# Odd layer's sample outputs in four column strips, with one transpose as a step of its own

## The reference

```python
def mix_odd(x, s_ret, start, w_in, w_out):
    z = x @ w_in
    q = rotate_xpos(z[..., :o1] ...); k = rotate_xpos(z[..., o1:o2] ...) * (DK_C ** -0.5)
    v = z[..., o2:o3].reshape(B, L, H_C, DV_C); g = z[..., o3:]
    ...
    o, s_new = chunked_linear_attention(q, k, v, log_a, s_ret, RET_CHUNK)
    o = rms_norm(o).reshape(B, L, MIX_C) * jax.nn.silu(g)
    return o.astype(x.dtype) @ w_out, s_new
```

## Time and profile before

| | us |
|---|---|
| three runs | 1682.03, 1676.82, 1681.51 |
| median | 1681.51 |
| span of the profiled execution | 1678.0 |

### The profile page before, as it was taken

How to read it: one execution, slowest core, us unless ns; L and a number is a source line. 1 busy time by engine, 2 the same in 40 slices (tenths; PEclk the granted TensorE clock), 3 DMA queues, 4 the chain that set the end, 5 groups by cost and what they waited for, 6 DMA issues and landing times.

```text
span 1678.0 us, 21821 instructions
## 1 busy us (share of the span) xinstructions
PE 1597.4 (95%) x7950; PEld 808.1 (48%) x7950; DVE 539.5 (32%) x1320; ACT 340.2 (20%) x689; POOL 144.5 (9%) x221
## 2 busy tenths in 40 slices
PE   8999899999999999999999999989999999999998
PEld 5784544434444443446665755554443444443343
DVE  2235622222222222351343335371222222222225
ACT  2101222211112211231222222012122112221122
POOL 0330100000000000000011011010000000000000
PEclk9969999999999999999999999989999999999999
DMA  9623789999989999953465586587999998999970
GB/s 301 241 82 133 276 335 419 420 420 420 420 354 420 420 420 420 383 205 134 163 238 207 183 282 219 191 322 292 420 421 420 420 419 357 422 420 421 419 294 29
DMA packets 119270, 536.09 MB, mean 319 GB/s; under 512 B 17848, under 2 KB 29368, under 8 KB 69407
## 3 DMA queue, kind: packets, MB, share of 16 engines
q1 hardware_dynamic: 95975, 470.35, 69.8%
q0 software_dynamic: 21360, 61.64, 10.2%
q10 hardware_dynamic: 1872, 3.22, 0.5%
HBM read 526.15 MB, written 23.87 MB: 328 GB/s over the span
## 4 chain that ended last, share of the span: by engine, by line
PE 82%; DMA 11%; DVE 3%; issue 2%; ACT 1%; SPq 1%; POOL 0%; ACTq 0%; DVEq 0%
PE ps L1244 23%; PE ps L1108 12%; PE ps L1086 12%; DMA weights<-in_w_exp_up 11%; PE ps L1258 10%; PE ps L1220 5%; PE ps L1237 3%; PE ps L1216 2%; PE ps L1251 1%; PE ps L1008 1%; PE ps L1097 1%; PE ps L1278 1%; PE ps L986 1%; PE ps L899 1%; PE ps L999 1%
## 5 line engine op out<-in xcount | busy, mean ns | idle before, releaser
L1244 PE MATMUL ps<-weights,x_feat 128*64 128x512 f32 x1984 | 437.8, 593 | 36.5 <-DMA weights<-in_w_exp_up 18.1
L1244 PEld LDWEIGHTS ps<-weights,x_feat 128*64 128x64 f32 x1984 | 147.1, 137 | 320.5 <-issue 317.9
L1258 PE MATMUL ps<-weights,arena 128*64 128x512 f32 x992 | 226.5, 598 | 0.9 <-ACT arena L1442 0.9
L1086 PE MATMUL ps<-x_feat,weights 128*128 128x288 f32 x832 | 211.3, 413 | 1.1 <-ACT x_feat L1442 1.1
L1086 PEld LDWEIGHTS ps<-x_feat,weights 128*128 128x128 f32 x832 | 161.1, 195 | 45.2 <-issue 3.2
L2089 DVE CAST split<-state 128x1024 fp32r<-128x1024 f32 (+1 forms) x66 | 44.8, 678 | 325.2 <-ACT state L1442 325.2
L2086 DVE SCALAR_TENSOR_TENSOR arena<-arena,ps 128x256 f32<-128x256 f32 x64 | 30.8, 481 | 364.3 <-ACT arena L1668 364.3
L2408 POOL DMA_INDIRECT arena<-x_rows,arena x64 | 63.4, 991 | 891.0 <-DVE arena L2079 845.5
L1442 ACT ACTIVATE state<-ps 128x512 f32<-128x512 f32 x132 | 78.8, 597 | 268.4 <-PE ps L1258 261.1
L1108 PE MATMUL ps<-weights,x_feat 128*128 128x512 f32 x288 | 127.0, 596 | 3.0 <-ACT x_feat L1468 3.0
L1258 PEld LDWEIGHTS ps<-weights,arena 128*64 128x64 f32 x992 | 65.7, 136 | 132.2 <-issue 130.9
(11 more groups left out here) (286 smaller groups left out, 1297.9 us busy)
## 6 DMA issues: line engine op xcount, KB each, us to landing
weights<-in_w_exp_gate SPq DMA_DIRECT2D x124, 1024.0 KB
weights<-in_w_exp_up SPq DMA_DIRECT2D x124, 1024.0 KB
weights<-in_w_exp_down SPq DMA_DIRECT2D x124, 1024.0 KB
weights<-in_w_in_c SPq DMA_DIRECT2D x24, 1024.0 KB
arena<-in_state_ret POOLq DMA_DIRECT2D x20, 512.0 KB, 5.5
out_ret_sample<-arena POOLq DMA_DIRECT2D x20, 512.0 KB, 7.0
weights<-in_w_in_a SPq DMA_DIRECT2D x8, 1024.0 KB
weights<-in_w_ple_gate SPq DMA_DIRECT2D x8, 1024.0 KB
```

The lines of the kernel that those rows point to most:

```text
L1086: last = pe.matmul(ps[:, 0:T], lhs(c), XT[:, c, :], start=(c == 0), stop=(c == n - 1))
L1244: last = pe.matmul(ps[64 * s:64 * s + 64, :], XGT[u][:, c, 64 * s:64 * s + 64], rhs, start=(c == 0), stop=(c == KC - 1))
L1258: last = pe.matmul(ps[64 * s:64 * s + 64, :], HT[u][:, c, 64 * s:64 * s + 64], wd[s][:, c, 512 * n:512 * n + 512], start=(c == 0), stop=(c ...
```

## The change

The sample's outputs are formed token-major first. The scores (128 rows by 32) and `fold4` (128 x 32) become the stationary operands, V and O4 the moving ones, 128 columns at a time; the four feature blocks go to four strips of 32 partitions of one bank (group `roS`). ScalarE copies these 128 x 128 into `O4[:, 0:128]`. A new step `outt` transposes them once on TensorE into the group `roTs`, and what ScalarE and VectorE did in `outs` they now do in `outt`. Because the scores are now read over all 128 rows, VectorE clears rows 32 to 127 of them once at the layer's start, and TensorE waits for that. `rest` has ten steps in place of nine, so that the dealing out moves some of the others too: for heads 0 to 2 the order is now qkh 0, qkh 1, state, qkh 2, outp, qkh 3, seqs 0, vstrips, norm 0, vv 0, seqs 2, vv 2, vv 1, seqs 4, gg 0, seqs 6, gg 1, outs, gg 2, outt, gg 3, norm 1 (before: ..., vstrips, vv 0, norm 0, vv 2, seqs 2, vv 1, seqs 4, gg 0, gg 1, seqs 6, gg 2, outs, gg 3, norm 1). The round of banks shifts by one group a head.

```diff
-            rest += [("outs", h - 1, 0), ("norm", h - 1, 1)]
+            rest += [("outs", h - 1, 0), ("outt", h - 1, 0), ("norm", h - 1, 1)]
...
-    steps += [("oute", 0, 1), seqs[2], ("oute", 1, 1), ("oute", 2, 1), seqs[3], ("out", 0, 0), ("outs", h, 0)]
+    steps += [("oute", 0, 1), seqs[2], ("oute", 1, 1), ("oute", 2, 1), seqs[3], ("out", 0, 0), ("outs", h, 0), ("outt", h, 0)]
...
                 elif kind == "outs":
+                    g.append(("roS", h))
+                elif kind == "outt":
                     g.append(("roTs", h))
...
                     emptied(pe, ("vv", h, 2))
                     emptied(pe, ("o4", h))
-                    ps = begin(("roTs", h))[:, 0:4 * TS].rearrange("p (f t) -> p f t", f=4)
-                    for f in range(4):
-                        vf = slice(P * f, P * f + P)
-                        pe.matmul(ps[:, f, :], V[0:TS, 2, vf], RAT[0:TS, SEQ + P:SEQ + P + TS], start=(f == 0), stop=False,
-                                  skip_group_check=True)
-                        last = pe.matmul(ps[:, f, :], O4[:, vf], fold4, start=False, stop=(f == 3), skip_group_check=True)
-                    end(last, ("roTs", h))
+                    pe.wait_ge(sem("sample_rows_cleared"), 1)
+                    ps = begin(("roS", h))
+                    for q in range(4):
+                        pe.matmul(ps[TS * q:TS * q + TS, 0:P], RAT[:, SEQ + P:SEQ + P + TS], V[:, 2, P * q:P * q + P],
+                                  start=True, stop=False)
+                    for q in range(4):
+                        last = pe.matmul(ps[TS * q:TS * q + TS, 0:P], fold4, O4[:, P * q:P * q + P], start=False, stop=True)
+                    end(last, ("roS", h))
+                elif kind == "outt":
+
+                    emptied(pe, ("roS", h))
+                    ps = begin(("roTs", h))
+                    end(pe.transpose(ps[:, 0:P], O4[:, 0:P], ident), ("roTs", h))
...
                         elif kind == "outs":
+                            full(act, ("roS", h))
+                            st.free(copy(O4[:, 0:P], bank(("roS", h))[:, 0:P]), ("roS", h))
+                        elif kind == "outt":
                             full(act, ("roTs", h))
...
             dve.wait_ge(sem("odd_in"), 16)
+            st.after
+            for r in (32, 64):
+                st.run(dve.memset(RAT[r:2 * r, SEQ + P:SEQ + P + TS], 0.0))
+            st.after.nop().then_inc(sem("sample_rows_cleared"), 1)
...
-                elif kind in ("outp", "outs"):
+                elif kind in ("outp", "outt"):
```

More of the change, by code:

```diff
@@ L267 @@
                ("pg", "fold", 0): 0, ("pg", "fold", 1): 4, ("pg", 1, 0): 5, ("pg", 1, 1): 6}
-ODD_GROUPS = ("qkh", "vv", "vstrips", "gg", "ratt", "kT", "kTs", "roT", "roTs", "sn", "sp", "rms", "out1", "oute1")
+ODD_GROUPS = ("qkh", "vv", "vstrips", "gg", "ratt", "kT", "kTs", "roT", "roS", "roTs", "sn", "sp", "rms", "out1", "oute1")
 def plan_groups():
```

## The result

The changed kernel takes 1670.44 us (median of 4 runs, 1669.34 to 1671.61) against 1680.82 us for the kernel before (median of 4 runs). The ratio is 0.993 with a 95% interval of 0.9915 to 0.9944: faster by 0.7%. The two medians lie 10.4 us apart, and 8.0 were forecast.

The account below looks back on a forecast made before the run. TensorE, busy 95% of the 1678.0 us span, was taken as the bound. Instructions 5.4 + 1.25 - 0.36 = 6.3 us plus 1.7 of clock gave 8.0 us, so a median of 1673.5 us, range 1668.5 to 1679.5.

Parts of the forecast that it names:

- the instructions: Odd layer's heads and router: 5.4 us from three heads plus 1.25 from the last, less 0.36 at the router: 6.3 us.
- the clock: Behind head 1's old products the clock fell to 0.50; expected to go with those products, saving another 1.7 us.
- Strips: Sample outputs of each head: 16 strip passes at 0.027 us plus 0.15 us fixed, 0.59 us in all.
- rival of strips in sequence: Sample outputs: strips don't run side by side, 4.5 us against 2.59 a head, 1689 us in all; chance 0.06.
- Transpose in the flow: Heads 0 to 2: a single transpose between dense products takes 0.20 us, with ends 0.14 and 0.44.
- Last head: outt directly behind outs, TensorE waits for ScalarE's copy: 1.34 us against 2.59, 1.25 saved.
- Bank of the second list: Router behind the layer: the second list falls on sh 3's bank and waits for VectorE, +0.36 us.
- Ring of states: Sequence states' loads in the heads: some 5 us earlier because norm 0 moves, so no stall at seqs 6.
- rival with a half-lost gain: Ring or a bank makes seqs 6 wait, 1.3 us in each of three heads: 1677.4 to 1679.1 us; chance 0.17.
- Experts: Expert weight stream behind the heads starts when the first expert products free panels, so the whole gain reaches the end.
- rival that kept the clock drop: Heads of the odd layer: the drop stays or lands elsewhere, only 6.3 us gained, 1675.2 us; chance 0.27.

Follow-up runs that it names:

- The two repeats: The kernel before and the changed kernel, each run again without edit: mean 1682.8 us, ratio 0.9999, and mean 1671.7 us, ratio 0.9939.
- the doubled products: Kernel before with its 16 sparse sample-output passes a head issued twice: mean 1703.1 us, ratio 1.0117.
- V first: Kernel before with all eight passes of V issued first, then all eight of O4, V still with 32 rows: mean 1674.5 us, ratio 0.9947.
- all rows twice: Kernel before with its old products over all 128 rows of V and the scores, issued twice: mean 1683.9 us, ratio 0.9997.
- all rows once: Kernel before with its old products over all 128 rows of V and the scores in place of 32, issued once: mean 1674.0 us, ratio 0.9949.

## Why the prediction was right, and where its sizes were off

The forecast was 1673.5 us in a range of 1668.5 to 1679.5; 1670.4 were measured. Sign, range and the mechanism hold; both parts of the sum came out too small, the instructions with 6.3 us against 7.6 and the clock with 1.7 against 3.7 in the mean of many runs.

- Strips: 0.59 us forecast, 0.58 measured, and the strips issued five times confirm the 0.027 us a pass. A line that already has the very form (L1103) was the right source. The rival of strips in sequence is out by this.
- Transpose in the flow: 0.20 forecast, 0.11 measured, below my lower end of 0.14, since the pair of the earlier trace rows contains the start behind a wait: in head 0, where no wait stands before them, the same two transposes of the kernel before take 0.22 us (800.99 to 801.21). Saved a head 1.90, not 1.80. (By the ends of this term the three heads give 4.7 to 5.6 us, not 5.4 with 0.7 to either side.)
- Last head: 1.25 forecast, 1.39 measured (1.20 us left in place of 1.34); the wait for ScalarE is there, with 0.40 us and not the 0.6 that I expected.
- Bank of the second list: +0.36 forecast. TensorE's wait grew from 0.29 to 0.74 us there. But behind the last head I had only this term, and the stage came out 0.57 us shorter beyond the sample outputs' 1.39, not 0.36 longer; this is the largest miss among the instructions. From `xTb`'s last transposes to the first expert product it took 38.9 us against 39.4 before, because less of the half-clock stretch around the router fell on products: those of L1178 and L1183 took 0.72 us less. The two repeats show the same (2.02 us in the kernel before, 1.38 in the changed one). Why the clock falls earlier there is open. I hadn't worked it out, so this part of the agreement was luck.
- Ring of states: no wait at `seqs 6`, the load 4.75 us earlier counted from the head's start (842.39 - 802.47 against 846.04 - 801.37). The rival with a half-lost gain is out.
- Experts: the first expert product starts 8.2 us earlier and the stage behind it takes 540.0 us against 540.6, so the whole gain reaches the end although the weights come at 420 GB/s.
- The clock is the term that was mis-sized most. I took the one drop of one profile, 1.7 us. The mechanism was right, as the doubled products show, but the number of drops differs by execution, and that profile had a low number. Over 37 runs of it, beside all experiments but V first and all rows twice, the kernel before gives away 31.4 us on average (32.4 in the 14 runs beside those two), and the changed kernel in nine runs 27.7: 3.7 us, a bit over two drops. This carries most of the difference between the forecast 8.0 and the means of those runs (1682.8 and 1671.1, 11.7 us; on one chip side by side 1682.4 and 1671.7, 10.7 us): 9.3 - 1.7 = 7.6 us between the anchors without the drop, and 3.7 of clock, 11.3 in all. The three profiles with the old products show one, three and one drops, 2.8 us on average; that the whole 3.7 lie behind the sample outputs is argued and not shown. The two profiles alone hide this: they differ by 8.8 us, near the forecast 8.0, because the kernel before happened to show one drop there too.
- The rule that a clock is lost in idle gaps between bursts (the Trainium skill, "TensorE: Matmul & The Clock Gate", "Why this matters for your kernels") doesn't cover this case: behind the sample outputs the clock fell while TensorE was recorded busy throughout. Idle time isn't the only thing that costs the clock. The rival that kept the clock drop (1675.2) is out by the profiles: five of them with strips show no drop in any head. Its time lies above every run of the changed kernel, but so does my forecast's, so the times alone don't decide.

What I had not asked: why a pass cost 0.162 us at all. I priced the removed step from its rows without splitting it. Reading all 128 rows, or issuing V's products first, gains 8 to 9 us where the change gains 11, without strips. Of instructions they save only 3.5 and 2.7 us against 7.6; the rest goes with the clock, behind the products and, as the profiles show, elsewhere too.

## What to carry to other kernels

Before a small step is rebuilt, split its price: here each change between a 32-row and a 128-row stationary cost 0.11 us, and avoiding most of them by one more loop gained 9.4 us, nearly as much as the whole rebuild (10.7 us side by side with the kernel before), though only 2.7 us of it are instructions and the rest goes with the clock. When a clock drop of 1.7 us shows behind some instructions in one profile, take its frequency from several profiles and from the mean clock of many runs, not from that profile's count. A step dealt into a list moves its neighbours and everybody's bank: write out each group's predecessor, since one new wait, or three old ones that can go, can be found on paper. Then look at what the removed wait had covered: in the last head 0.71 of 1.18 us came back on another engine.

## What the runs showed of the hardware

- TensorE's granted clock can fall to 0.50 (1.2 GHz) although the engine is recorded busy throughout. It did so right behind the old sample products in 5 of 12 heads (three profiles), in two of four heads of all rows twice and in four of four of the old products twice. It did in no head of the kernels with all rows once, with all of V first, and with strips, the strips five times among them. Each short drop costs 1.7 us (5.66 against 3.98 us for the next dense step).
- A change between a 32-row and a 128-row stationary costs about 0.11 us (2.59, 1.91 and 1.71 us for 16 passes with eight, two and no changes).
- Strips of a 128x32 stationary with 128 moving columns, four to a bank, cost 0.027 us a pass (1.74 us for 64 more passes).
- A single f32 transpose of 128x128 between dense products costs 0.11 us (862.21 to 862.32).
- ScalarE loads the table of its next function ahead of that function's wait (load at 864.18, function at 866.25, behind a wait of 0.79 us for TensorE).
